# Every second SwiGLU block of the first feed-forward part turned by VectorE instead of TensorE

## The reference

```python
def swiglu(h, w_in, w_out):
    gate, up = jnp.split(h @ w_in, 2, axis=-1)
    return (jax.nn.silu(gate) * up) @ w_out

def sandwich(x, fn, g_pre, g_post, shift, scale, gate, res_w):
    h = rms_norm(x, g_pre) * (1.0 + scale[:, None]) + shift[:, None]
    y = rms_norm(fn(h), g_post)
    return x + res_w * gate[:, None] * y
```

## Time and profile before

| | us |
|---|---|
| median of 3 runs | 1907.82 (1907.48 to 1907.96) |
| the profiled execution | 1910.38 |
| its span, first to last instruction | 1908.6 |
| TensorE matmul busy in the span | 1864.7 (98%) |
| VectorE busy | 1470.7 (77%) |
| ScalarE busy | 857.9 (45%) |
| GpSimd busy | 82.0 (4%) |

### The profile page before, as it was taken

One profiled execution on the slowest core, in us unless ns is written; L12 is line 12 of the kernel. 1 busy time (PEld: TensorE's weight loads), 2 busy tenths in 40 slices (PEclk: granted clock), 3 DMA queues, 4 the chain that ended last, 5 costly groups with the idle time before them and its releaser, 6 DMA issues.

```text
span 1908.6 us, 21980 instructions
## 1 busy us (share of the span) xinstructions
PE 1864.7 (98%) x8775; PEld 1567.9 (82%) x8775; DVE 1470.7 (77%) x1569; ACT 857.9 (45%) x1095; POOL 82.0 (4%) x151
## 2 busy tenths in 40 slices
PE   6999999999999999999999999999999999999997
PEld 6887888888888889878888887888888888888895
DVE  5988889798888889965776587677867785676576
ACT  4244443443443434574666545544344434443443
POOL 0001000000000000010000010000000000000000
PEclk9999999999999999999999999999999999999999
DMA  9999999999999989655444444766677655556552
GB/s 368 374 370 343 355 340 342 353 333 348 347 341 346 371 325 347 247 165 176 146 133 133 160 155 151 246 242 235 234 250 251 240 180 198 197 191 213 177 202 77
DMA packets 208677, 486.84 MB, mean 255 GB/s; under 512 B 8560, under 2 KB 29760, under 8 KB 193472
## 3 DMA queue, kind: packets, MB, share of 16 engines
q1 hardware_dynamic: 191648, 365.72, 55.3%
q0 software_dynamic: 16224, 117.47, 16.7%
q10 hardware_dynamic: 704, 2.25, 0.3%
HBM read 483.31 MB, written 2.10 MB: 254 GB/s over the span
## 4 chain that ended last, share of the span: by engine, by line
PE 91%; DVE 4%; DMA 2%; issue 1%; ACT 1%; ACTq 0%; SPq 0%; DVEq 0%; POOL 0%
PE ps_u L1551 10%; PE ps_u L1553 10%; PE ps_u L1552 10%; PE ps_g L1551 9%; PE ps_g L1553 9%; PE ps_g L1552 9%; PE ps_t L1551 4%; PE ps_t L1553 4%; PE ps_t L1552 4%; PE ps_y L1553 4%; PE ps_y L1552 4%; PE ps_y L1551 4%; DVE arena L1267 1%; PE ps_g L1649 1%; PE ps_t L1820 1%
## 5 line engine op out<-in xcount | busy, mean ns | idle before, releaser
L595 ACT ACTIVATE w_hi<-w_raw 128x1024 fp32r<-128x1024 f32 (+2 forms) x604 | 629.0, 1043 | 881.2 <-PE ps_u L1553 308.5
L977 DVE TENSOR_TENSOR w_lo<-w_raw,w_hi 128x1024 fp32r<-128x1024 f32 (+2 forms) x604 | 719.7, 1200 | 356.5 <-ACT w_hi L595 354.4
L1551 PE MATMUL ps_u<-w_hi,xT_hi 128*128 128x512 f32 (+2 forms) x880 | 345.1, 392 | 4.0 <-DVE arena L1033 1.8
L1553 PE MATMUL ps_u<-w_hi,xT_lo 128*128 128x512 f32 (+2 forms) x880 | 339.4, 386 | 0.0
L1552 PE MATMUL ps_u<-w_lo,xT_hi 128*128 128x512 f32 (+2 forms) x880 | 338.9, 385 | 0.0
L1551 PE MATMUL ps_g<-w_hi,xT_hi 128*128 128x512 f32 (+1 forms) x816 | 319.1, 391 | 0.5 <-DVE w_lo L977 0.4
L1553 PE MATMUL ps_g<-w_hi,xT_lo 128*128 128x512 f32 (+1 forms) x816 | 314.6, 386 | 0.0
L1552 PE MATMUL ps_g<-w_lo,xT_hi 128*128 128x512 f32 (+1 forms) x816 | 314.1, 385 | 0.0
L1011 DVE SCALAR_TENSOR_TENSOR arena<-ada_raw,cond,arena 128x2048 f32<-128x2048 f32 x108 | 253.4, 2347 | 4.6 <-DMA ada_raw<-in_ada_w 4.5
L1551 PEld LDWEIGHTS ps_u<-w_hi,xT_hi 128*128 128x128 f32 x880 | 165.5, 188 | 35.8 <-DVE arena L1033 2.2
L1553 PEld LDWEIGHTS ps_u<-w_hi,xT_lo 128*128 128x128 f32 x880 | 165.6, 188 | 32.2
(11 more groups left out here) (316 smaller groups left out, 1905.5 us busy)
## 6 DMA issues: line engine op xcount, KB each, us to landing
w_raw<-in_ffn_w_in SPq DMA_DIRECT2D x157, 1024.0 KB, 6.6
ada_raw<-in_ada_w POOLq DMA_DIRECT2D x112, 1024.0 KB, 6.2
w_raw<-in_ffn_w_out SPq DMA_DIRECT2D x80, 1024.0 KB, 6.5
w_raw<-in_mix_w_in SPq DMA_DIRECT2D x32, 1024.0 KB, 5.1
ada_raw<-in_ada_w SPq DMA_DIRECT2D x32, 512.0 KB, 8.9
arena<-in_ada_w SPq DMA_DIRECT2D x32, 512.0 KB, 9.6
w_raw<-in_mix_w_out SPq DMA_DIRECT2D x16, 1024.0 KB, 5.0
w_raw<-in_ffn_w_in SPq DMA_DIRECT2D x16, 768.0 KB, 5.4
```

The source lines that it names most:

```text
L595: nc.scalar.activation(w_hi[:, u % 4, 0:n, 0:width], w_raw[:, s, 2 * hf:2 * hf + n, 0:width], ACT.Copy).then_inc(hi_done, 3 if g in EARLY_ ...
L977: nc.vector.tensor_tensor(w_lo[:, u % 4, 0:n, 0:width], w_raw[:, s, 2 * hf:2 * hf + n, 0:width], w_hi[:, u % 4, 0:n, 0:width].bitcast(F32) ...
L1551: nc.tensor.matmul(o, a_hi[:, k, rows], w_hi[:, b, c, 0:width], start=start, stop=False)
L1553: ins = nc.tensor.matmul(o, a_lo[:, k, rows], w_hi[:, b, c, 0:width], start=False, stop=stop)
```

## The change

`on_vector(j)` names the blocks that VectorE turns. It is true for all but the last block of the second part, as before, and now also for blocks 1, 3, 5, 7 and 9 of the first part (turned in passes 2, 4, 6, 8 and 10). For these the eight transposes of line 1615 are left out, the 16 of line 1056 are put behind units 3 to 6 of the gate group, and the result goes to `spare`. Blocks 0, 2, 4, 6, 8 and 10 stay with TensorE.

```diff
+def on_vector(j):
+
+    f, i = divmod(j, FBLOCKS)
+    return i < FBLOCKS - 1 and (f == 1 or i % 2 == 1)
...
-        h_turned = acc[:, 1, 0:4 * SEQ].rearrange("p (c n) -> p c n", n=SEQ)
+        h_turned = [part.rearrange("p (c n) -> p c n", n=SEQ) for part in (spare[:, :], acc[:, 1, 0:4 * SEQ])]
...
-                    if FBLOCKS <= j < 2 * FBLOCKS - 1:
-                        nc.scalar.activation(dst[:, :, :], h_turned, ACT.Copy).then_inc(ht_hi_done, 1)
+                    if on_vector(j):
+                        nc.scalar.activation(dst[:, :, :], h_turned[j // FBLOCKS], ACT.Copy).then_inc(ht_hi_done, 1)
...
-                    if FBLOCKS <= j < 2 * FBLOCKS - 1:
-                        nc.vector.tensor_tensor(lo[:, :, :], h_turned, hi[:, :, :].bitcast(F32), ALU.subtract).then_inc(ht_lo_done, 1)
+                    if on_vector(j):
+                        nc.vector.tensor_tensor(lo[:, :, :], h_turned[j // FBLOCKS], hi[:, :, :].bitcast(F32), ALU.subtract).then_inc(ht_lo_done, 1)
...
-                        dst = h_turned[q * BLOCK:(q + 1) * BLOCK, :, :].rearrange("p c (t n) -> p t c n", n=P)
+                        dst = h_turned[j // FBLOCKS][q * BLOCK:(q + 1) * BLOCK, :, :].rearrange("p c (t n) -> p t c n", n=P)
...
-                    if f == 1:
+                    if on_vector(j0 + j - 1):
                         for rows in range(P // BLOCK):
                             parts[0].setdefault(3 + rows, []).append(turn_hidden(j0 + j - 1, rows))
...
-                    if f == 0:
+                    if not on_vector(j0 + j - 1):
                         transpose_h(j0 + j - 1, 4, y0 + 4 * (j - 1))
```

## The result

The changed kernel takes 1911.27 us (median of 15 executions, 1909.03 to 1914.67) against 1907.82 (15, 1907.02 to 1911.61): ratio 1.0017, interval 1.001 to 1.0024, that is 1.9 to 4.6 us slower. The profiled execution's span grew only from 1908.6 to 1910.1.

A forecast was written before the change was run, and what follows sets the result against it. TensorE was taken to bound the kernel (91% of the span). −1.4 us for passes 2, 4, 6, 8 and +6.6 for pass 10 gave +5.2 on the median 1907.82: 1913.0 us, range 1909.3 to 1916.0.

The forecast's parts named there:

- Passes 2, 4, 6, 8: First part: transposes leave TensorE, late low parts take some back; gain 0.36 us a pass, −1.4 us for four.
- second restart: Gate group of passes 2, 4, 6, 8: another TensorE pipeline restart, lower bound of the gain, 0.2 us a pass.
- Pass 10, gate group: VectorE's quarters make TensorE wait before units 5, 6, 7; the up group starts 4.9 us late.
- Pass 10, up group: A tile waits for its transfer, 7.5 us after the buffer comes free; TensorE resumes 6.6 us late.
- lower bound of 5.3: Pass 10: smallest loss forecast, in us, from the shortest tile transfer of the stretch, 5.8, plus 0.4 to issue it.
- (a): Rival, pass 10: TensorE's clock falls too after its waits, +1.6 us, 1914.6 us; chance 0.19.
- (b): Rival: four full savings of 0.9 us (−3.7), pass 10 at +5.3 by the quickest transfer; +1.6, 1909.4 us; chance 0.22.
- (c): Rival: cheap transposes in the four quarters, 2.5 us a block; −1.4 in sum, 1906.4 us; chance 0.07.
- the trace disagrees: VectorE's transposes: 7.5 us a block in fp32 by the trace, against 2.5 us from the skill page's bf16 figure.
- (d): Rival, pass 10: tile transfers at 9.3 us and a clock fall, +9.0 us, 1916.8 us; chance 0.04.

The follow-up runs named there:

- late_quarters: Kernel before with blocks 1, 3, 5, 7 turned by VectorE, quarters behind units 3, 4, 6, 7 of the gate group: 1904.95 us, ratio 0.9983.
- short_tiles: Changed kernel with adaLN tiles from number 87 on multiplying only 256 of 2048 columns: 1907.07 us, ratio 0.9993 to the kernel before.
- gain_late: Changed kernel with the gate's scaling moved from pass 10's gate group to behind unit 6 of its up group: 1909.1 us, ratio 1.0009 to the kernel before.
- changed_again: The changed kernel timed and profiled once more, nothing altered: 1910.5 us, ratio 1.0017 to the kernel before.

## Why the prediction was right, and where its sizes were off

**Right in sign and inside its range** (1909.3 to 1916.0), for the reason given: four passes gain little because VectorE delays the last units of the gate group, and pass 10 loses more than all gain. The forecast was +5.2 us, the median moved +3.45, the passes +2.8. By the passes the forecast was nearly twice too large, and it is partly luck that the median came out nearer to it. I gave 0.69 to a change of over 0.2%; at 0.17% (0.10 to 0.24) it is most likely below that line.

**Passes 2, 4, 6, 8.** The walk had low part 6 done at 16.35, level with TensorE, unit 7 at 19.48 us and the up group at 22.32; measured are unit 6 at 16.41, unit 7 at 19.49 and the up group at 22.37. Unit 6 was so just late enough for the second restart, which I had only in the bounds. Gain forecast 0.36 a pass, measured 0.29 to 0.32 in three. Pass 6 gained 0.94, which I had missed: there the third tile is the first of its adaLN row, a plain multiply, and takes 1.19 from its start to the next instruction instead of 2.26. VectorE's timeline in pass 6 of the changed kernel:

```profile
463.95 1.28 DVE L1015 TENSOR_SCALAR arena<-ada_raw,cond 128x2048 f32<-128x2048 f32 x1
465.14 1.77 DVE L1062 STREAM_TRANSPOSE spare<-arena 32x256 f32<-32x256 f32 x4
```

That one microsecond less on VectorE removes the lateness shows the cause a second time, beside late_quarters. Sum forecast −1.4, measured −1.8.

**Pass 10, gate group.** Units 5, 6, 7 and the up group were forecast 12.24, 17.29, 20.11 and 22.31 us into the pass; measured 12.26, 17.31, 20.12, 22.32. The waits too (1.8, 2.85 and 0.6 idle, against 1.67, 2.67 and 0.44 in brackets, which count from the modelled end of the last matmul).

**Pass 10, up group: the term that was mis-sized.** I took 7.5 us from the end of a tile to the start of the one two further on, and so +6.6. Measured, from 751.43 (where the tile frees the buffer) to 757.16 are 5.73, and VectorE wasn't waiting for the transfer even then: 5.73 is its own work in between, four low parts and a tile. The transfer that decides, issued at 751.81, landed 5.1 us later; before, the one issued at 747.59 took 8.0. I had argued that the transfers would be less crowded, since the weight loads also come later, and then took only a little off. The trace fits that: while it was in flight (751.80 to 757.00) the DMA engines were busy 0.79 of the time; before (747.60 to 755.60) it was 0.98. The transfer's time left the sum, and VectorE's own work, which I had not set against it, took its place. With 5.73, 754.78 + 5.73 + 4.37 = 764.88 and +4.8; measured at the down group 39.63 us into the pass against 34.75 (the row of before is below), +4.88. It lies under my lower bound of 5.3, for which I had used the quickest transfer of before, 5.8, when crowding itself was what would change.

```profile
766.42 0.39 PE L1551 MATMUL ps_y<-w_hi,hT_hi 128*128 128x512 f32 x1
```

**The rivals.** (a): the clock did fall in pass 10 in two of the three profiles that have these waits, but behind the 2.7 us wait only, and hid behind VectorE; the 1.6 us were not paid. (b) had the quick transfer right and the full savings wrong in three passes of four; its figure, 1909.4, was 1.9 too low, mine 1.7 too high. By the passes (+2.8) it was the nearer of the two, +1.6 against my +5.2. (c): a quarter costs 1.8 us in `spare` too, so transposes are not cheap here. Its 2.5 us a block came from a bf16 figure for a 128x128 square; these are float32, 32 partitions an instruction, so my "the trace disagrees" set unlike things side by side, and only the 7.5 us is shown. (d) is out: the deciding transfer took 5.1 us, not 9.3.

The odd passes were 0.06 us shorter in several profiles and not in others (68.00 to 68.01 in short_tiles and gain_late); I have no cause for it.

## What to carry to other kernels

Work moved to an engine with free time is only free where the engine's queue has lead at that place: walk the queue instruction by instruction over the one group in which it lands, against the times at which the bounding engine wants each result. Do it for every stage in which the edit acts; here one narrow stage out of five, where the tiles kept their size while the units shrank, turned a gain of 1.8 us into a loss. The repair was to leave that stage alone, put two quarters one place later, and turn eight blocks instead of five: 1900.07 us and, measured again, 1901.1, where the kernel before takes 1907.7 and the changed one 1910.5 to 1911.3.

## What was not expected of the hardware

After a wait of nearly the same length (1.77 and 1.70 us at the same place) the granted clock fell to half in one execution and stayed full in another; after 2.67 us in pass 10 it fell in one profile (0.50 in the window shown) and stayed at 1.00 in the changed kernel's first, whose window behind that wait is below. It also fell after 2.69 (changed_again) and 2.43 us (gain_late), and in none of the three profiles with a wait of 1.67 us before unit 5 did it fall behind that one.

```profile
746.00:748.00 2.00, 1.99 (x12) 1.67 (x10) 1.93 (x5) 0.00 (x0) 0.00 (x0) 1.00 0.71 299
```

A single profile thus can't say whether such a wait costs the clock, and spans of single profiles can differ by about 1.6 us for this alone (an estimate: eight matmuls at 0.43 instead of 0.23 us behind 148.63 in the kernel before).
